# Weight columns packed and streamed in reverse order in a float32 two-block transformer kernel

## What is computed

```python
def swiglu(h, w_gate, w_up, w_down):
    a = jnp.einsum('bsd,df->bsf', h, w_gate)
    u = jnp.einsum('bsd,df->bsf', h, w_up)
    return jnp.einsum('bsf,fd->bsd', jax.nn.silu(a) * u, w_down)
...
proj = jnp.einsum('bsd,dk->bsk', h, w_in)
...
return jnp.einsum('bsd,de->bse', merged, w_out)
```

## Time and profile before

| | |
|---|---|
| median of 3 runs | 2814.52 us (2813.97 to 2814.7) |
| span of the profiled execution | 2812.3 us |
| TensorE matmuls busy | 2792.6 us, 99% of the span, 15556 matmuls |
| TensorE weight loads busy | 2396.6 us, 85% |
| VectorE busy | 1921.3 us, 68% |
| ScalarE busy | 1554.0 us, 55% |
| GpSimd busy | 241.5 us, 9% |
| read from device memory | 500.12 MB, 178 GB/s over the span |

### The profile page before, as it was taken

One profiled execution on the slowest core, in us unless ns is written; L12 is line 12 of the kernel. 1 busy time (PEld: TensorE's weight loads), 2 busy tenths in 40 slices (PEclk: granted clock), 3 DMA queues, 4 the chain that ended last, 5 costly groups with the idle time before them and its releaser, 6 DMA issues.

```text
span 2812.3 us, 40293 instructions
## 1 busy us (share of the span) xinstructions
PE 2792.6 (99%) x15556; PEld 2396.6 (85%) x15556; DVE 1921.3 (68%) x3180; ACT 1554.0 (55%) x2718; POOL 241.5 (9%) x187
## 2 busy tenths in 40 slices
PE   9999999999999999999999999999999999999998
PEld 8889888888889888888888987888888888878887
DVE  6756676747655667756568777776566687777765
ACT  6545656545545656545456556455455465655553
POOL 0010011010010011010014100110100141001100
PEclk9999999999999999999999999999999999999999
DMA  6544445555544345555554344555555554445553
GB/s 242 191 171 158 149 156 182 193 185 190 195 167 152 139 172 194 199 190 195 195 193 179 136 163 159 210 194 182 199 189 195 183 187 153 158 156 184 209 185 135
DMA packets 75055, 503.82 MB, mean 179 GB/s; under 512 B 8784, under 2 KB 10480, under 8 KB 19184
## 3 DMA queue, kind: packets, MB, share of 16 engines
q1 hardware_dynamic: 74576, 501.07, 50.2%
q10 hardware_dynamic: 288, 0.17, 0.0%
HBM read 500.12 MB, written 1.08 MB: 178 GB/s over the span
## 4 chain that ended last, share of the span: by engine, by line
PE 93%; DVE 4%; POOL 2%; issue 1%; ACT 1%; DMA 0%; SPq 0%; DVEq 0%; ACTq 0%
PE ps L1544 45%; PE ps L1579 21%; PE ps L1585 11%; PE ps L1563 9%; PE ps L1606 3%; POOL wlo L2498 2%; DVE wlo L2038 1%; PE ps L1701 1%; PE ps L1699 1%; DVE conv L2327 1%; PE ps L1726 1%; PE ps L1716 0%; PE ps L1717 0%; PE ps L1718 0%; DVE ps L2144 0%
## 5 line engine op out<-in xcount | busy, mean ns | idle before, releaser
L1777 ACT ACTIVATE whi<-raw 128x1024 fp32r<-128x1024 f32 (+3 forms) x938 | 977.5, 1045 | 600.3 <-PE ps L1544 426.1
L2038 DVE TENSOR_TENSOR wlo<-raw,whi 128x1024 fp32r<-128x1024 f32 (+2 forms) x894 | 1084.1, 1220 | 219.9 <-ACT whi L1777 218.9
L1579 PE MATMUL ps<-xT_both,whi 128*128 128x512 f32 x2560 | 641.6, 393 | 0.0
L1544 PE MATMUL ps<-whi,xT_both 128*128 128x512 f32 (+2 forms) x2336 | 628.9, 391 | 2.6 <-DVE xT_both L2061 1.6
L1579 PEld LDWEIGHTS ps<-xT_both,whi 128*128 128x128 f32 x2560 | 461.1, 189 | 82.6
L1544 PEld LDWEIGHTS ps<-whi,xT_both 128*128 128x128 f32 x2336 | 425.5, 188 | 83.7 <-issue 9.3
L1585 PEld LDWEIGHTS ps<-xT_both,wlo 128*128 128x128 f32 x2560 | 349.3, 191 | 24.9
L1585 PE MATMUL ps<-xT_both,wlo 128*128 128x256 f32 x2560 | 357.1, 282 | 0.0
L1544 PE MATMUL ps<-wlo,xT_both 128*128 128x512 f32 (+2 forms) x1168 | 354.6, 385 | 0.3 <-DVE wlo L2038 0.3
L2118 DVE TENSOR_TENSOR h<-h,ps 128x256 f32<-128x256 f32 x320 | 127.0, 418 | 203.1 <-ACT h L1826 203.1
L1544 PEld LDWEIGHTS ps<-wlo,xT_both 128*128 128x128 f32 x1168 | 218.4, 188 | 43.7 <-DVE wlo L2038 1.4
(11 more groups left out here) (315 smaller groups left out, 2526.7 us busy)
## 6 DMA issues: line engine op xcount, KB each, us to landing
raw<-in_w SPq DMA_DIRECT2D x435, 1024.0 KB, 4.8
vr<-in_vrows SPq DMA_DIRECT2D x19, 512.0 KB, 5.6
raw<-in_w SPq DMA_DIRECT2D x12, 768.0 KB, 4.3
raw<-in_w SPq DMA_DIRECT2D x10, 896.0 KB, 4.5
sums<-scratch SPq DMA_DIRECT2D x8, 512.0 KB, 4.4
raw<-in_w SPq DMA_DIRECT2D x4, 832.0 KB, 4.4
raw<-in_w SPq DMA_DIRECT2D x4, 576.0 KB, 3.7
raw<-in_w SPq DMA_DIRECT2D x4, 512.0 KB, 6.9
```

The source lines that it names most:

```text
L1544: made = e.matmul(bank[:, 0:c1 - c0], xs[:, kt, sl], ws[:, j * w + c0:j * w + c1], start=kt == 0 and n == 0, stop=kt == job.nk - 1 and n == 2)
L1579: e.matmul(bank[:, :].rearrange("p (n x) -> p n x", n=2), hi[:, o:o + 128], job.xt.both[:, :, kt, :], start=kt == 0, stop=False, skip_grou ...
L1777: e.activation(out, raw, ACT.Copy).then_inc(*mark("hi", i))
L2038: e.tensor_tensor(out, raw, hi.bitcast(F32), sub).then_inc(*mark("lo", i))
```

## The change

The matmul of `rows` reads its moving operand, the weight columns, through a view with a step of minus one: it begins at the last address of the run of columns and ends at the first. So that the same column comes out at the same place, the host packs these columns in reverse order: for a piece that goes through `rows`, each run of `min(width, 512)` columns is turned around. Pieces whose weights stand (`STANDING`, and the `up` chunks past the first) are packed as before. The number of matmuls, their sizes, the order of the steps on every engine, the waits, the placing of buffers, the bytes loaded and the output's layout in PSUM are as they were; in the built program the operand `[step 1, 512 elements]` from element 512 of `wlo` reads `[step -1, 512 elements]` from element 1023, and so for every matmul of `rows`.

```diff
+STANDING = ("qk1", "xbc", "qc", "kc", "dt")
+
+
+def backward(key, width):
+    standing = key[3] > 0 if key[1] == "up" else key[0] in STANDING
+    return 0 if standing else min(width, 512)
...
-                    made = e.matmul(bank[:, 0:c1 - c0], xs[:, kt, sl], ws[:, j * w + c0:j * w + c1],
+                    made = e.matmul(bank[:, 0:c1 - c0], xs[:, kt, sl], ws[:, j * w + c0:j * w + c1][:, ::-1],
                                     start=kt == 0 and n == 0, stop=kt == job.nk - 1 and n == 2)
...
-            _, width, kts = pieces[i]
+            key, width, kts = pieces[i]
+            first, turn = off, backward(key, width)
             for idx, kt, ranges in kts:
                 for name, c0, c1 in ranges:
                     dst[:, off:off + c1 - c0] = a[name][idx][128 * kt:128 * kt + 128, c0:c1]
                     off += c1 - c0
+            if turn:
+                cut = dst[:, first:off].reshape(128, -1, turn)
+                dst[:, first:off] = cut[:, :, ::-1].reshape(128, -1)
```

## The result

| | before | after |
|---|---|---|
| median of the runs | 2814.49 us | 2846.97 us |
| span of the profiled execution | 2812.3 us | 2845.3 us |
| TensorE matmuls busy | 2792.6 us | 2826.7 us |
| the changed matmuls alone (6216) | 1435.9 us | 1470.2 us |

The change makes the kernel slower by 32.5 us, a ratio of 1.0115 (95% interval 1.0103 to 1.0127). In the changed kernel all lines past the new functions stand 8 lines further down: L1544 is L1552 now, L1579 and L1585 are L1587 and L1593, L1777 and L2038 are L1785 and L2046.

What follows compares the result with a forecast made beforehand. TensorE's matmuls, by the distance between starts at line 1544, were taken as the bound. All terms were 0, so the 2812.3 us span plus 2.2 us around it gave 2814.5 us; range 2786 to 2871 us.

Steps and rivals of the forecast that it cites:

- a rival to which I gave 0.12: The dearer start, whose upper price of 2871 us was the top of the stated range.
- The bound and the place: TensorE's matmuls cover 99% of the span; what matters is the distance between starts at line 1544, 226.7 ns for 512 columns.
- The fixed terms: Host packing, loads, splitting instructions, instruction order, waits and the PSUM write were all said to be unchanged: 0 us.
- I take 0: Reading the moving operand of line 1544's 6216 matmuls in reverse costs 0 us, between bounds of -135 and +1301 us.
- the wide matmul: Matmul streaming two runs of 256 columns with an address jump between, 227.5 ns each; taken as nearest evidence for no cost.
- The dearer start: Each matmul of line 1544 starts a few ns later, the same for all widths: +36 to +56 us, 2851 to 2871 us; chance 0.12.
- a dearer column: Sign to look for at line 1544: an added amount that goes with the number of columns streamed.
- Faster: Reversing avoids the moving read meeting the next stationary operand's load in memory: -26 us, 2788 us; chance 0.12.
- the fixed part: Time in every matmul beyond its streamed columns, 13.4 ns at 512 columns, said to be the same at 512, 384 and 256.
- Half pace: Descending columns stream at half the rate in every matmul of line 1544, 440 ns between starts: +1301 us, 4116 us; chance 0.13.
- The row that was to show half pace: The plain float32 product, read as two matmuls of 256 columns in 0.44 us, 0.86 ns a column.
- the 13.4 ns: What is left of 226.7 ns for a 512-column matmul after 213.3 ns of streaming; 83 us over 6216 matmuls.

## Why the prediction was wrong

The forecast was 2814.5 us, no change; 2846.97 us came out. The time lies in the stated range only because that took in the price of a rival to which I gave 0.12, and that rival's mechanism is not the one the runs show.

- *The bound and the place.* Right. The time is TensorE's distance between starts, L1544 and nothing else moved, and no cover hid it: 34.3 us of busy time in that line, 32.5 us in the total.
- *The fixed terms* (packing, order, waits, splitting, the write to PSUM): right, all at 0. VectorE and ScalarE are busy as long as before.
- *"I take 0".* This is the step that failed: the term for the direction of the moving operand, put at nothing, measured +34.3 us in L1544, 6.6 ns for 512 columns. It rested on the wide matmul, whose streamed operand jumps between two runs at full pace, and on the argument that a step of minus one touches the same words equally often. The first is what that one matmul shows, and the second is arithmetic; neither says that order is free. The runs show that the order of 16-, 64- and 128-byte groups inside 256 bytes costs (233.4, 233.4 and 232.4 ns) and that the order of 256-byte blocks doesn't (226.8). What I left out beside it is the second read at the same time, the load of the next stationary operand, which moves the upward stream from 226.8 to 232.3 ns. The jump in the wide matmul is of 8192 bytes, a whole number of 256-byte units, so it keeps the place in the unit, just as the blocks of 256 bytes do, which cost nothing either. The row that I took for the nearest was the one case that could not show the effect.
- *The dearer start.* The price came near, by luck, and the mechanism is wrong. I had +36 us for 5.8 ns on every matmul, taken from the distances after transposes; +32.5 us was measured. I had also said how to tell them apart: a dearer start costs every width the same, a dearer column costs an amount that goes with the columns. The loss is 0.2 ns with 288 columns, 3.6 with 384, 4.4 with 416 and 6.5 with 512, so it isn't the same amount; in the earlier trace rows it is 5.0 ns for 384 columns and in the earlier trace rows 6.6 for 512, both 0.013 ns a column. The runs say it too: 256-byte blocks begin far up in the run and cost nothing.
- *Faster.* I had thought here of the streamed read and the load meeting in memory, which the runs bear out for the upward stream, but with the wrong sign for this change, and priced only what would be gained. I argued it away with the fixed part being equal at 512, 384 and 256 columns, "where the reads stand in different relation". As far as their starts go they don't: in the trace of the kernel before nearly all loads begin 2 to 5 ns after their matmul, at each of these widths, so the equal fixed part spoke for nothing. And a part of it can be had back: with xT moved by 192 bytes the matmuls of 256 columns take 114 ns, 7 ns above 256 x 0.417, where I had found 12.
- *Half pace.* Out: 233.3 ns, not 440. The row that was to show half pace says less than I took from it: each product of L1737 is one call with 256 columns, made four times, and the trace has eight records of it. So the 0.44 us of the earlier trace rows is one product in two records, and they don't show how fast a column enters.
- *The reading of the code.* The kernel lays its activation buffers at the same place modulo 256 bytes as the weight buffers (`lined`). That was a sign in the code that place matters to something, and the edit changed the place at each moment of the stream. It should have had a term in the sum.

The Trainium skill, "SBUF — State Buffer", section "Specifications (TRN2)", has the rule on lines of 16 bytes that the prediction weighed. The order within 16 bytes being free (2814.53 us) agrees with it; what it would make of the whole change, which is nothing, does not, and the measurement decides. The Trainium skill, "TensorE: Matmul & The Clock Gate", section "Step-by-step: what each phase is for", says that loading the next tile's weights doesn't take read bandwidth from the running matmul. Here the runs differ from it in effect: with the streamed read unchanged to the address, moving the loaded operand by 128 bytes took the distance from 226.8 to 232.3 ns.

What stays open: why the downward stream has 233.3 ns at all four places, and beside a load that doesn't walk. That its reader alone pays for descending groups inside 256 bytes isn't excluded; that only the mean, and not the single distances, is the same with the load 128 bytes further speaks against it being the whole account. A downward stream beside a load that walks the other way than it does here wasn't tried. That the two reads compete for parts of memory that repeat every 256 bytes is argued, not seen: the trace shows starts, not reads. Nor is it shown how much of the 13.4 ns is of this kind with 512 columns, or why 288 columns lose nothing.

## What to carry to other kernels

In this kernel TensorE is the bound and each matmul has its own load. There the place of the streamed operand and of the operand loaded beside it, counted modulo 256 bytes, was worth up to 10 ns of 227 ns, and 1 to 2% of the whole. In a kernel of this kind it is worth trying the places 0, 64, 128 and 192 bytes for each large buffer, and judging by the distance between starts. Reversing the columns inside 16 bytes, or the order of whole blocks of 256 bytes, was free; reversing the order of groups of 16, 64 or 128 bytes was not. A tile that is streamed in one product and stands in another can have two best places, as xT has here, and the sum decides. When two theories differ in how a cost goes with the width, read it at every width that the kernel has.

## What the hardware showed that I had not expected

- Four bytes of shift in the weight buffers cost 48.3 us (2862.73 us against 2814.48), more than reversing the whole stream.
- The same 258 matmuls took 58.51, 59.77, 59.94, 60.20, 60.78 or 61.07 us in one piece without a break, by the addresses and the order of the two reads alone.
- In the downward stream the load's place changed the single distances, from 233 and 234 ns to 231, 232 and 235, and left their mean at 233.4.
- One activation buffer moved by 192 bytes made the kernel before 0.4% faster (2802.79 us against 2814.07).
